# Moving the split operands of a Trainium2 kernel to multiples of 64 bytes

## The reference

```python
# first block, two layers (one recurrent, one with differential attention)
h = rms_norm(x, pre_norm[l]);  mem_n = rms_norm(mem, mem_norm[l])
proj = h @ w_in                       # z or q, gate, q_mem, g_mem
y_br = rwkv7_time_mix(...)            # layer 0
y_br = diff_attention(q, k_sh, v_sh)  # layer 1, k_sh, v_sh = rms_norm(x, kv_norm) @ w_kv
y_mem = memory_cross_attention(q_mem, mem_n, w_mem_kv[l])
y = concat(y_br * silu(gate), y_mem * silu(g_mem)) @ w_out[l]
x = x + rms_norm(y, post_norm[l])
# second block, 16 meta tokens ahead of the 256
h = h + 0.5 * swiglu(rmsnorm(h, ffn1_norm), w_gate, w_up, w_down)      # inner width 2816
h = h + hybrid_mixer(rmsnorm(h, mix_norm), ...)   # retention, indexed top-k attention, gates
h = h + 0.5 * swiglu(rmsnorm(h, ffn2_norm), w_gate, w_up, w_down)
return rmsnorm(h, final_norm)[:, 16:]
```

## Time and profile before

| | |
|---|---|
| median of 3 runs | 1263.34 us (1263.26 to 1264.85) |
| the profiled execution | 1266.96 us, span 1265.2 us |
| mean granted TensorE clock | 0.976 |
| TensorE busy | 94% of the span, 9718 matmuls |
| VectorE, ScalarE, GpSimd busy | 67%, 50%, 14% |
| moved by DMA | 186.83 MB, mean 148 GB/s |

### The profile page before, as it was taken

How to read it: one execution, slowest core, us unless ns; L and a number is a source line. 1 busy time by engine, 2 the same in 40 slices (tenths; PEclk the granted TensorE clock), 3 DMA queues, 4 the chain that set the end, 5 groups by cost and what they waited for, 6 DMA issues and landing times.

```text
span 1265.2 us, 23933 instructions
## 1 busy us (share of the span) xinstructions
PE 1187.7 (94%) x9718; PEld 1141.0 (90%) x9718; DVE 847.5 (67%) x1456; ACT 627.1 (50%) x1076; POOL 180.4 (14%) x186
## 2 busy tenths in 40 slices
PE   6978699888987899999999999999999999999997
PEld 4978687788987899999989999999999999999997
DVE  6778854776766676655487755779556668877642
ACT  6865353664555554444243345543445445655441
POOL 1127130200003021110122000013000001212101
PEclk9999799999997899999999999999999999999999
DMA  7333211343452565556335542345554345866560
GB/s 253 127 126 116 86 58 35 126 146 112 137 164 88 191 207 176 170 153 187 109 130 188 166 150 84 117 148 171 166 176 161 126 157 174 257 187 186 161 202 34
DMA packets 53677, 186.83 MB, mean 148 GB/s; under 512 B 6720, under 2 KB 8896, under 8 KB 53184
## 3 DMA queue, kind: packets, MB, share of 16 engines
q1 hardware_dynamic: 53008, 183.07, 45.2%
q10 hardware_dynamic: 560, 2.24, 0.5%
HBM read 184.24 MB, written 1.05 MB: 146 GB/s over the span
## 4 chain that ended last, share of the span: by engine, by line
PE 82%; DVE 10%; ACT 4%; issue 1%; DMA 1%; POOL 0%; DVEq 0%; SPq 0%; ACTq 0%; POOLq 0%
PE bank L2617 22%; PE bank L2620 22%; PE bank L2618 22%; DVE wl L2052 3%; PE bank L2634 2%; PE bank L2978 1%; PE bank L2635 1%; PE bank L2638 1%; ACT wh L1679 1%; PE bank L2657 1%; PE bank L2602 1%; DVE zl L2159 1%; PE bank L2666 1%; DMA raw<-w_a_w_in 1%; DVE sqr L2163 1%
## 5 line engine op out<-in xcount | busy, mean ns | idle before, releaser
L2052 DVE TENSOR_TENSOR wl<-raw,wh 128x1024 fp32r<-128x1024 f32 (+1 forms) x343 | 423.9, 1245 | 192.8 <-ACT wh L1679 189.3
L2617 PE MATMUL bank<-xh,wh 128*128 128x256 f32 (+1 forms) x1880 | 543.2, 289 | 1.9 <-ACT wh L1679 1.6
L2620 PE MATMUL bank<-xh,wl 128*128 128x256 f32 (+1 forms) x1880 | 536.2, 285 | 6.4 <-DVE wl L2052 6.3
L2618 PE MATMUL bank<-xl,wh 128*128 128x256 f32 (+1 forms) x1880 | 536.0, 285 | 0.0
L1679 ACT ACTIVATE wh<-raw 128x1024 fp32r<-128x1024 f32 (+1 forms) x343 | 355.1, 1044 | 272.6 <-PE bank L2620 260.4
L2617 PEld LDWEIGHTS bank<-xh,wh 128*128 128x128 f32 x1880 | 359.3, 191 | 7.4 <-issue 3.6
L2620 PEld LDWEIGHTS bank<-xh,wl 128*128 128x128 f32 x1880 | 357.6, 190 | 8.2 <-DVE wl L2052 8.0
L2618 PEld LDWEIGHTS bank<-xl,wh 128*128 128x128 f32 x1880 | 357.3, 190 | 0.5
L2618 PE MATMUL bank<-hl,wh 128*128 128x272 f32 (+1 forms) x352 | 99.9, 284 | 0.0
L2620 PE MATMUL bank<-hh,wl 128*128 128x272 f32 (+1 forms) x352 | 99.9, 284 | 0.0
L2617 PE MATMUL bank<-hh,wh 128*128 128x272 f32 (+1 forms) x352 | 99.9, 284 | 0.0
(11 more groups left out here) (379 smaller groups left out, 1716.9 us busy)
## 6 DMA issues: line engine op xcount, KB each, us to landing
raw<-w_ffn_gate SPq DMA_DIRECT2D x44, 512.0 KB, 4.2
raw<-w_ffn_up SPq DMA_DIRECT2D x44, 512.0 KB, 4.2
raw<-w_a_w_in SPq DMA_DIRECT2D x29, 512.0 KB, 3.5
raw<-w_ffn_down SPq DMA_DIRECT2D x32, 448.0 KB, 3.5
raw<-w_w_out SPq DMA_DIRECT2D x16, 512.0 KB, 3.5
raw<-w_b_w_in SPq DMA_DIRECT2D x16, 512.0 KB, 4.6
raw<-w_ffn_down SPq DMA_DIRECT2D x16, 512.0 KB, 3.7
raw<-w_ret SPq DMA_DIRECT2D x16, 512.0 KB, 3.5
```

The costliest lines, as they stand in the source:

```text
L2052: v.tensor_tensor(lo[:, c], raws[n % N_RAW][:, c], hi[:, c].bitcast(F32), ALU.subtract).then_inc(*w_lo.up(n))
L2617: pe.matmul(ps, hi[:, c], x_hi(k), start=(k == 0), stop=False)
L2618: pe.matmul(ps, hi[:, c], x_lo(k), start=False, stop=False)
L2620: last = pe.matmul(ps, lo[:, c], x_hi(k), start=False, stop=(k == kt - 1))
```

## The change

The tensors of SBUF are put in another order and padded differently. `xh` and `xl` become [128, 8, 256] tensors of the scope `first`, used by the two layers. The later phases get tensors of their own, `x2h` and `x2l` of 2560 columns: 272-column operands there are eight rows of 1280 bytes, 256-column ones eight rows of 1024 bytes that start 192 bytes in. The hidden layer of the first feed-forward has rows of 1280 bytes instead of 1536. `cols`, `ed_end` and the pad tensors move or change size. No instruction is added or taken away.

Worked out from the sizes, where the split operands start (bytes in the partition; remainder by 64; distance of the rows):

| operand | before | after |
|---|---|---|
| weights `wh0`, the others multiples of 4096 on in the ring | 74720, 32 | 57312, 32 |
| extra weight buffers of layer 1, ffn1, ffn2 | 32 | 32 |
| `xh`, `xl` in the layers | 30368 and 39072, 32, rows 1024 | 81920 and 90112, 0, rows 1024 |
| `mh`, `ml` (memory, layer 0) | 32, rows 1024 | 32, rows 1024 |
| `mh1`, `ml1` (memory, layer 1), `kh`, `kl` | 32, rows 1024 | 0, rows 1024 |
| ffn1 and mix, 272 columns | 30368 and 39072, 32, rows 1088 | 96768 and 107008, 0, rows 1280 |
| mixq, 256 of them | 64 bytes further, 32, rows 1088 | 64 bytes further, 0, rows 1280 |
| ya, ffn2, 256 columns | 30368 and 39072, 32, rows 1024 | 96960 and 107200, 0, rows 1024 |
| `hh`, `hl` of ffn1 | 32, rows 1536 | 0, rows 1280 |
| `hh`, `hl` of ffn2 | 32, rows 1024 | 0, rows 1024 |
| `yh`, `yl` | 32, rows 1024 | 0, rows 1024 |

```diff
         res = sb("res", [P, KT, T])
+        cols = sb("cols", [P, NCOL])
         ta = sb("ta", [P, W_A])
-        xh, xl = sb("xh", [P, KT, T], dt=F32R), sb("xl", [P, KT, T], dt=F32R)
-        cols = sb("cols", [P, NCOL])
...
         first = ExitStack()
+        sb("before_x", [P, 8], first)
+        xh, xl = sb("xh", [P, KT, S], first, F32R), sb("xl", [P, KT, S], first, F32R)
...
         ed = sb("ed", [P, BT, 2, CH + 1], ph)
-        ed_end = sb("ed_end", [P, BT], ph)
-        sb("after_ed", [P, 104], ph)
...
         mrs = sb("mrs", [P, MEM], ph)
+        ed_end = sb("ed_end", [P, BT], ph)
...
-        sb("space", [P, 624], ph)
+        sb("space", [P, 744], ph)
...
         tb = sb("tb", [P, W_B])
+        sb("before_x2", [P, 8])
+        x2_hi, x2_lo = (sb(n, [P, 2560], dt=F32R) for n in ("x2h", "x2l"))
+        rows = lambda buf, at, row, n: buf[:, at:at + KT * row].rearrange("p (k t) -> p k t", k=KT)[:, :, 0:n]
+        hi_of = {S: rows(x2_hi, 48, S, S), T: rows(x2_hi, 0, 320, T)}
+        lo_of = {S: rows(x2_lo, 48, S, S), T: rows(x2_lo, 0, 320, T)}
...
-            sb(f"before_hid{n}", [P, 64], ph)
-            row = -(-FFN_TOK[n] // P) * P
-            hid[n] = [sb(f"h{part}{n}", [P, FT, row], ph, F32R)[:, :, 0:FFN_TOK[n]] for part in "hl"]
-            sb(f"after_hid{n}", [P, 80], ph)
+            sb(f"before_hid{n}", [P, {1: 16, 2: 32}[n]], ph)
+            n_tok, row = FFN_TOK[n], {1: 320, 2: 256}[n]
+            hid[n] = [sb(f"h{part}{n}", [P, FT, row], ph, F32R)[:, :, 0:n_tok] for part in "hl"]
+            sb(f"after_hid{n}", [P, {1: 120, 2: 104}[n]], ph)
...
-        sb("before_y", [P, 8])
+        sb("before_y", [P, 24])
...
-            "h0": (lambda k: hi_of[S][:, k, :], lambda k: lo_of[S][:, k, :], in_lo, "h0"),
+            "h0": (lambda k: xh[:, k, :], lambda k: xl[:, k, :], in_lo, "h0"),
...
-            "ffn1": (lambda k: xh[:, k, :], lambda k: xl[:, k, :], in_lo, "ffn1"),
+            "ffn1": (lambda k: hi_of[T][:, k, :], lambda k: lo_of[T][:, k, :], in_lo, "ffn1"),
...
-                        s.activation(hi_of[T - lo][:, i, :], res[:, i, lo:T], ACT.Copy, scale=col(tag, i)).then_inc(
+                        s.activation((hi_of[T] if layer else xh)[:, i, :], res[:, i, lo:T], ACT.Copy, scale=col(tag, i)).then_inc(
```

More of the change, by code:

```diff
@@ L550, in build @@
             "mem1": (lambda k: mh1[:, k, :], lambda k: ml1[:, k, :], in_lo, "mem1"),
[L551 to L553 removed]
+            "h0": (lambda k: xh[:, k, :], lambda k: xl[:, k, :], in_lo, "h0"),
+            "y0": (lambda k: xh[:, k, :], lambda k: xl[:, k, :], in_lo, "y0"),
+            "pre1": (lambda k: xh[:, k, :], lambda k: xl[:, k, :], in_lo, "pre1"),
             "kvn": (lambda k: kh[:, k, :], lambda k: kl[:, k, :], in_lo, "kvn"),
[L555 to L556 removed]
+            "y1": (lambda k: xh[:, k, :], lambda k: xl[:, k, :], in_lo, "y1"),
+            "ffn1": (lambda k: hi_of[T][:, k, :], lambda k: lo_of[T][:, k, :], in_lo, "ffn1"),
             "hid1": (lambda k: hid[1][0][:, k, :], lambda k: hid[1][1][:, k, :], f_lo, 1),
[L558 to L559 removed]
+            "mix": (lambda k: hi_of[T][:, k, :], lambda k: lo_of[T][:, k, :], in_lo, "mix"),
+            "mixq": (lambda k: hi_of[T][:, k, QS], lambda k: lo_of[T][:, k, QS], in_lo, "mix"),
             "yg": (lambda k: yh[:, k, :], lambda k: yl[:, k, :], in_lo, "yg"),
@@ L2105, in vector_program @@
                             on.wait_ge(*in_hi.past(("h0", k)))
-                            v.scalar_tensor_tensor(lo_of[S][:, k, :], sq_x[:, k, :], col("pre0", k),
-                                                   hi_of[S][:, k, :].bitcast(F32), ALU.mult, ALU.subtract).then_inc(
+                            v.scalar_tensor_tensor(xl[:, k, :], sq_x[:, k, :], col("pre0", k),
+                                                   xh[:, k, :].bitcast(F32), ALU.mult, ALU.subtract).then_inc(
                                 *in_lo.up(("h0", k)))
@@ L2276, in vector_program @@
                     on.wait_ge(*in_hi.past(("y0", j)))
-                    v.tensor_tensor(lo_of[S][:, c, :], qm0[:, :, :] if j == 3 else pair(ysb, j),
-                                    hi_of[S][:, c, :].bitcast(F32), ALU.subtract).then_inc(*in_lo.up(("y0", j)))
+                    v.tensor_tensor(xl[:, c, :], qm0[:, :, :] if j == 3 else pair(ysb, j),
+                                    xh[:, c, :].bitcast(F32), ALU.subtract).then_inc(*in_lo.up(("y0", j)))
                 elif kind == "branch":
@@ L2288, in vector_program @@
                         on.wait_ge(*in_hi.past(("y1", k)))
-                        v.tensor_tensor(lo_of[S][:, k, :], rh1[:, k, :] if k < BT else qm1[:, k - BT, :],
-                                        hi_of[S][:, k, :].bitcast(F32), ALU.subtract).then_inc(*in_lo.up(("y1", k)))
+                        v.tensor_tensor(xl[:, k, :], rh1[:, k, :] if k < BT else qm1[:, k - BT, :],
+                                        xh[:, k, :].bitcast(F32), ALU.subtract).then_inc(*in_lo.up(("y1", k)))
                 elif kind == "mo_evac":
@@ L2307, in vector_program @@
                     lo, tag = MO[layer][2:4]
+                    hi, lo_ = (hi_of[T], lo_of[T]) if layer else (xh, xl)
                     for i in (k, k + 1):
                         on.wait_ge(*in_hi.past((tag, i)))
-                        v.scalar_tensor_tensor(lo_of[T - lo][:, i, :], res[:, i, lo:T], col(tag, i),
-                                               hi_of[T - lo][:, i, :].bitcast(F32), ALU.mult, ALU.subtract).then_inc(
+                        v.scalar_tensor_tensor(lo_[:, i, :], res[:, i, lo:T], col(tag, i),
+                                               hi[:, i, :].bitcast(F32), ALU.mult, ALU.subtract).then_inc(
                             *in_lo.up((tag, i)))
```

9 lines of the change are left out of this document (3 added, 6 removed).

## The result

The changed kernel is slower: 1273.54 us (1271.9 to 1274.46, four runs) against 1263.3 (1261.8 to 1264.85, four runs), 10.2 us between the medians; the estimated ratio is 1.0073 (95% interval 1.0051 to 1.0094), which is 9.2 us (6.4 to 11.9). The forecast was 1236 us, faster, with an own range of 1230 to 1241; the wider range went from 1200 to 1280.

A forecast was written before the change was run, and what follows sets the result against it. TensorE's start-to-start time in split matmuls was taken as the bound. The parts summed to 23.4 to 31.6 us saved, middle 27.5: 1266.96 − 27.5 − 3.6 = 1235.9, so 1236 us, own range 1230 to 1241.

The forecast's parts named there:

- What bounds the kernel: Whole kernel: TensorE, busy 94% of the span; from 421 us on the time between matmul starts counts.
- Part (2): 256-column later phases: moving rows 32 bytes off the weights' remainder by 64 bring the fast level, 9.1 + 6.2 us saved.
- Rival A: All split matmuls: the penalty goes altogether as 17 pieces of 64 bytes become 16; 57.6 us saved, 1206 us, chance 0.22.
- Part (1): 272-column matmuls of the first feed-forward and mixer: rows of 1280 bytes save 6.1 us, up to 12.6 + 1.7.
- Part (3): The two layers' 1944 split matmuls: slow ones reach the fast level, 4 us, half hidden by other engines, 2 us saved.
- E: Every split matmul: half-piece distance makes reads collide, 38 us slower or half of it, 1282 to 1301 us, chance 0.20.
- D: All split matmuls settle on the slow level, fast stretches go; net nothing, 1263 us, chance 0.10.
- C: Position within 64 bytes does nothing, only even rows pay: 6.1 us saved, 1257 us, chance 0.12.

The follow-up runs named there:

- the map: No model, only streams of 256-column split-like matmuls, eight moving starts (xa to xh, 0 to 224 bytes) against eight weight starts: 113.3 to 120.0 ns by distance.
- the maps of 272 columns: No model, only streams of 272-column split-like matmuls at various row lengths and distances from the weights; rows of 1280 bytes took 123.3 to 126.7 ns.
- the kernel with even rows: Changed kernel with all operands 192 bytes from the weights modulo 256, rows of 1280 bytes, mixer's rows at 160: 1255.05 us, ratio to before 0.9924.
- the two new traces of before: The kernel before, with nothing changed, traced two more times: 1269.41 and 1264.27 us.

## Why the prediction was wrong

*What bounds the kernel* was right: the 10 us are in the time from one matmul's start to the next, from 421 us on no wait of TensorE changed by more than half a microsecond, and the counts stayed.

*Part (2), the 32 bytes between the reads,* is the step that failed. I took two reads in step for the worst case, and half a piece of 64 bytes apart for the cure, and called before's distance "in step". It isn't: the period is 256, not 64, and before's 192 bytes is the best distance on the map, with 113.3 in 12 of 16 streams there (64, once at 117.8 throughout and once at 113.3, is the other with these two levels). By the remainder of 64 the change moved everything by 32 bytes; modulo 256 it went from 192 to 32, 96, 224 or 64, stage by stage, which the prediction never worked out. What I read as a fault of the layout (two levels) was its merit: at the new distances the fast one was gone. The forecast gave 9.1 + 6.2 us to this part; measured, the 256-column stages of the later phases lost 5.0 us.

*Rival A* rested on 113.2 ns being 17 pieces of 16 columns. With moving rows on a multiple of 64 (xa, xe and xg of the map), 16 pieces, the best is the same 113.3. The 17 was a coincidence, and no stream in any of the maps went below 113.3.

*Part (1), even rows,* had half of the mechanism and the wrong size: in the maps of 272 columns rows of 1280 bytes take 123.3 to 126.7 ns by their distance, on both sides of the walking rows' 126.1. I took 3.0 ns from the down-projection's row, which stood at distance 192 as well, while the change put these rows at 32: 0.3 ns, 0.6 us instead of 6.1 to 12.6. At 192 or 160 they do bring 2.4 to 2.7. The 528 of the down-projection, for which I counted 0 to 1.7 us gained, lost 1.2.

*Part (3), the layers:* I wrote 2 us gained; the starts cost 3.5 more, and at 421 us, where the layers end, the trace is 2.2 behind. That looks like the part hidden by other engines that I had counted on, but the two traces differ in the granted clock ahead of 421 us too (0.96 and 1.00 in 0 to 40 us, 1.00 and 0.93 in 155 to 180), so the hidden share is not shown.

*The rivals.* E was the right sign and the nearest mechanism, a worse distance between the two reads, with chance 0.20; its rule of half a piece was part (2)'s and wrong like it, and that the reads collide no run shows. Its price of 38 us came from another full step in every matmul; the mean loss is 9.2 / 8136 = 1.1 ns, a quarter of such a step. D had the loss of the fast stretches, but not the new values of 118.3 and 120.0. C, with 6.1 us, fails on the distance.

*The check of the working that was missing:* all even-row operands of before share one distance, so the earlier trace rows could not tell a good distance from a bad one. The only row with other distances was the walking one, which was the slowest of its size, 126.1 against 123.1. It could have said that other distances cost more, and I read it as the price of walking.

## What to carry to other kernels

With fp32r matmuls that load new weights each time, the address of the moving rows relative to the weights is worth 3 to 6% of the time of these matmuls (113.3 against 116.7 to 120.0 ns; 3% for 272 columns), so measure it as a map before choosing pads. Here 192 bytes modulo 256 was best for 256 columns, and 160, 192 or 240 with rows a multiple of 256 bytes for 272. When a trace shows two levels, first ask whether the other layouts have the better one at all. And before two medians are compared, look whether their executions had the same granted clock: here executions of one kernel that differ in it can be 5 to 7 us apart.

## What the runs showed of the hardware

- The time of a split matmul depends on the distance of moving rows and weights modulo 256 bytes, in steps as fine as 8 bytes: 113.3 ns at 192, 120.0 at 184 and 200, 121.1 at 72, where 256 columns at one for each period of 2.4 GHz would be 106.7. Alignment as such does nothing: rows at 0 and 32 past 64 are equal at equal distance (within 0.3 ns, but for 160, where single streams differ by up to 2.7). Why the period is 256, which unit the two reads share, if they share one, and whether the load that matters is that of the matmul itself or of the next, no run shows.
- "SBUF — State Buffer" of the Trainium skill (section on the DMA port swizzle) speaks of lines of 16 bytes; a rule on single lines would repeat every 16 bytes, and the map doesn't (120.0 at 0, 118.7 at 16, 116.8 at 32). "TensorE: Matmul & The Clock Gate" of the Trainium skill (section on the back-to-back issue gap) has N/2.4 + 2.5 ns for the gap of an isolated matmul, by which an estimate for 256 columns is 109.2 ns; no distance reached it.
- At 192 (and 64) a stream has two levels, 113.3 and 117.8 ns, and can keep the one it has for over a thousand matmuls (the second feed-forward: 1056 at 117.8 in the first trace of before). Which one it takes varies between executions in some stages (ya, mg, y0, y1) and not in others; two kernels with the same distances had the second feed-forward at 117.6 and 113.4. What decides is open.
- One kernel's executions spread over 7 to 8 us (1262.9 to 1270.0 for before in one session, 1250.9 to 1258.8 for the kernel with even rows). In the two new traces of before the gap of 5 us went with the granted clock in several stretches ahead of 430 us, 155 to 180 us among them (0.86 or 0.93), in layer 0's recurrence, where TensorE has pauses.
